# Fewer matmuls for the forget sums, a sixth PSUM bank for the odd projection, and a later wait for parameters in a hybrid encoder trunk

## What is computed

```python
logf = jax.nn.log_sigmoid((f_logit + b_f).astype(jnp.float32))
c_all = jnp.cumsum(jnp.concatenate([flogf_past.astype(jnp.float32), logf], axis=1), axis=1)
c_keys = c_all.transpose(0, 2, 1)[:, :, None, :]
c_q = c_all[:, P:]

def block(qp, qb, cqb):
    s = jnp.einsum('bqhd,bkhd->bhqk', qb, k_all).astype(jnp.float32)
    s = s + cqb.transpose(0, 2, 1)[..., None] - c_keys
    s = jnp.where(qp[:, None] >= kpos[None, :], s, NEG_INF)
    p = jax.nn.softmax(s, axis=-1).astype(v_all.dtype)
    return jnp.einsum('bhqk,bkhd->bqhd', p, v_all)
```

## Time and profile before

| | |
|---|---|
| three timed runs, us | 2606.72, 2608.28, 2618.82 (median 2608.28) |
| the profiled execution, us | 2615.28 |
| its span, us | 2613.2 |
| TensorE busy, us | 2454.7 (94%) |
| VectorE busy, us | 1699.5 (65%) |
| ScalarE busy, us | 1206.8 (46%) |
| mean granted clock of TensorE | 0.972 |

### The profile page before, as it was taken

The page is one execution under the profiler, slowest core; times in us unless marked ns, Lnnn a source line. Parts: engine busy times, 40 slices in busy tenths (PEclk is TensorE's granted clock), DMA queues, the critical chain, the costliest instruction groups (busy, mean ns, idle before and its releaser), DMA issues.

```text
span 2613.2 us, 37692 instructions
## 1 busy us (share of the span) xinstructions
PE 2454.7 (94%) x13907; PEld 2190.8 (84%) x13907; DVE 1699.5 (65%) x2809; ACT 1206.8 (46%) x2239; POOL 118.5 (5%) x177
## 2 busy tenths in 40 slices
PE   5999999998899899999989999999988898999998
PEld 5999987977767799988789998877777577999887
DVE  6777647676555877754687775474235858777546
ACT  5545435344344555543555553453224655554444
POOL 1000001100001000000100000010000010000000
PEclk9999999999899899999989999999997999999999
DMA  4233234421303232234522333343343042223335
GB/s 127 80 90 89 97 129 161 114 69 49 106 1 117 66 93 82 82 113 136 169 66 82 92 87 113 129 157 97 105 125 114 1 142 68 81 82 95 99 128 177
DMA packets 259140, 261.89 MB, mean 100 GB/s; under 512 B 25568, under 2 KB 214000, under 8 KB 258977
## 3 DMA queue, kind: packets, MB, share of 16 engines
q1 hardware_dynamic: 254224, 243.83, 31.1%
q0 software_dynamic: 4464, 14.80, 1.6%
q10 hardware_dynamic: 288, 1.10, 0.1%
HBM read 249.11 MB, written 10.58 MB: 99 GB/s over the span
## 4 chain that ended last, share of the span: by engine, by line
PE 78%; DVE 12%; ACT 4%; issue 3%; DMA 1%; POOL 1%; ACTq 0%; DVEq 0%; SPq 0%; POOLq 0%
PE ps L845 13%; PE ps L847 13%; PE ps L846 13%; PE ps L903 5%; PE ps L905 5%; PE ps L904 5%; PE ps L1311 3%; PE ps L1313 2%; PE ps L1312 2%; PE ps L962 2%; PE ps L964 2%; PE ps L963 2%; PE ps L1797 1%; PE ps L1501 1%; DVE xb L708 1%
## 5 line engine op out<-in xcount | busy, mean ns | idle before, releaser
L845 PE MATMUL ps<-xb,w_all 128*128 128x320 f32 x2400 | 752.3, 313 | 50.1 <-DVE w_all L592 29.4
L846 PE MATMUL ps<-xb,w_all 128*128 128x320 f32 x2400 | 749.0, 312 | 0.0
L847 PE MATMUL ps<-xb,w_all 128*128 128x320 f32 x2400 | 748.8, 312 | 0.0
L845 PEld LDWEIGHTS ps<-xb,w_all 128*128 128x128 f32 x2400 | 457.0, 190 | 58.3 <-issue 43.2
L492 DVE TENSOR_TENSOR w_all<-raw,w_all 128x1024 fp32r<-128x1024 f32 (+1 forms) x204 | 207.8, 1020 | 393.9 <-ACT w_all L502 212.6
L846 PEld LDWEIGHTS ps<-xb,w_all 128*128 128x128 f32 x2400 | 457.3, 191 | 0.0
L847 PEld LDWEIGHTS ps<-xb,w_all 128*128 128x128 f32 x2400 | 457.1, 190 | 0.0
L486 ACT ACTIVATE w_all<-raw 128x1024 fp32r<-128x1024 f32 (+1 forms) x204 | 182.4, 895 | 477.5 <-PE ps L905 254.8
L592 DVE TENSOR_TENSOR w_all<-raw,w_all 128x512 fp32r<-128x512 f32 x404 | 277.9, 690 | 147.1 <-ACT w_all L585 146.1
L585 ACT ACTIVATE w_all<-raw 128x512 fp32r<-128x512 f32 x404 | 253.2, 629 | 182.5 <-PE ps L847 139.2
L903 PE MATMUL ps<-w_all 128*128 128x512 f32 x528 | 205.9, 390 | 1.0 <-DVE w_all L507 1.0
(11 more groups left out here) (357 smaller groups left out, 3989.9 us busy)
## 6 DMA issues: line engine op xcount, KB each, us to landing
raw<-in_w_ffn_out SPq DMA_DIRECT2D x176, 512.0 KB, 3.4
raw<-in_w_ffn_in SPq DMA_DIRECT2D x120, 512.0 KB, 5.1
gain<-in_w_ffn_in SPq DMA_DIRECT2D x56, 512.0 KB, 5.0
raw<-in_w_in_odd SPq DMA_DIRECT2D x56, 256.0 KB, 2.7
raw<-in_w_out_even SPq DMA_DIRECT2D x16, 512.0 KB, 3.5
raw<-in_w_out_odd SPq DMA_DIRECT2D x16, 512.0 KB, 3.5
gain<-in_norm_g POOLq DMA_DIRECT2D x12, 512.0 KB, 7.3
raw<-in_w_in_even SPq DMA_DIRECT2D x24, 256.0 KB, 2.6
```

Source lines behind the costliest of these rows:

```text
L845: nc.tensor.matmul(dst, wl, xh[:, k, :], start=first, stop=False, skip_group_check=True)
L846: nc.tensor.matmul(dst, wh, xl[:, k, :], start=False, stop=False, skip_group_check=True)
L847: mm = nc.tensor.matmul(dst, wh, xh[:, k, :], start=False, stop=(k == HK - 1), skip_group_check=True)
```

## The change

It has three parts. First, the wait for `par_done` moves from behind the parameters' transposes to the place in front of the turning of tile 3, which writes bank 7. Second, the odd projection's blocks take their banks in turn from six (bank 7 is added), so a tile waits for the copy of the tile six places before it instead of five, and the loops are written out. Third, the forget sums of a head are made per key block alone, four matmuls; the sum of the blocks in front comes as a bias when ScalarE copies bank 6, so that copy is cut into four. These sums of the blocks in front, `nc_before`, are made once for all heads, by six matmuls more in `pe_cumulate` and a second copy of VectorE.

```diff
-        O_BANK = [0, 1, 4, 3, 2]
+        O_BANK = [0, 1, 4, 3, 2, 7]
...
                 if i == AHEAD:
+                    if f == 0:
+                        pe.wait_ge(par_done, 1)
                     pe_xt(pe, pre_, 3, 3)
...
-        def block_bank(name, t):
-            return bank(O_BANK[t] if name == "OT" else t)
+        def block_bank(name, b, t):
+
+            return bank(O_BANK[(5 * b + t) % 6] if name == "OT" else t)
...
+            for b in range(blocks):
                 for k in range(KD):
                     u = block_unit(name, first + b, k)
-                    pe.wait_ge(lo_done, reg(slot_no(u) + 1, it, KD))
+                    pe.wait_ge(lo_done, slot_no(u) + 1)
                     for t in range(NT):
-                        if k == 0:
-                            free(t)
-                        mm = block_tile(name, u, it, k, t)
+                        if k == 0 and start and b == 0:
+                            start(t)
+                        elif k == 0:
+
+                            pe.wait_ge(t_out, t0 + 5 * b + t + 1 - (6 if name == "OT" else 5))
+                        mm = block_tile(name, first + b, u, k, t)
...
                             for kb in range(NP):
-                                for b in range(kb + 1):
-                                    mm = nc.tensor.matmul(bank(6, P, kb * P), lgn[:, b, h:h + 1].to_broadcast([P, P]),
-                                                          con[:, C_UT:C_UT + P] if b == kb else ones,
-                                                          start=(b == 0), stop=(b == kb))
+                                mm = nc.tensor.matmul(bank(6, P, kb * P), lgn[:, kb, h:h + 1].to_broadcast([P, P]),
+                                                      con[:, C_UT:C_UT + P], start=True, stop=True)
...
-                        nc.scalar.activation(negc[:, h % 2, :], bank(6), ACT.Copy).then_inc(nc_done, 1)
+                            act.wait_ge(cq_done, 1)
+                        nc.scalar.activation(negc[:, h % 2, 0:P], bank(6, P), ACT.Copy)
+                        for kb in range(1, NP):
+                            e = nc.scalar.activation(negc[:, h % 2, kb * P:(kb + 1) * P], bank(6, P, kb * P), ACT.Identity,
+                                                     bias=nc_before[:, kb - 1, h:h + 1])
+                        e.then_inc(nc_done, 1)
...
+            for i in range(1, NP):
+                for b in range(i):
+                    mm = nc.tensor.matmul(bank(7, NH, 96 + (i - 1) * NH), ones, lgn[:, b, :], start=(b == 0), stop=(b == i - 1))
             mm.then_inc(cq_mm, 1)
...
-                    nc.vector.tensor_copy(cq, bank(7, NP * NH, 64).rearrange("p (t h) -> p t h", h=NH)).then_inc(cq_done, 1)
+                    nc.vector.tensor_copy(cq, bank(7, NP * NH, 64).rearrange("p (t h) -> p t h", h=NH))
+                    nc.vector.tensor_copy(nc_before, bank(7, (NP - 1) * NH, 96).rearrange("p (t h) -> p t h", h=NH))\
+                        .then_inc(cq_done, 1)
...
                 mm.then_inc(par_ps, 1)
-                pe.wait_ge(par_done, 1)
```

More of the change, by code:

```diff
@@ L226, in build_trunk @@
         cq = view(small, 480, NP, NH)
+        nc_before = view(small, 232, NP - 1, NH)
         h0a = small[:, 320:328]
@@ L1301, in block_unit, with block_tile @@
             return UNITS[name] + b * KD + k + (KD if name == "OT" and b else 0)
-        def block_bank(name, t):
-            return bank(O_BANK[t] if name == "OT" else t)
[L1306 to L1310, removed]
+        def block_bank(name, b, t):
+            return bank(O_BANK[(5 * b + t) % 6] if name == "OT" else t)
+        def block_tile(name, b, u, k, t):
+            wh, wl = w_slot(u, None, BW)
+            xh, xl = xt_lhs(u, None, k, t)
+            dst = block_bank(name, b, t)
             nc.tensor.matmul(dst, xl, wh, start=(k == 0), stop=False)
@@ L1335, in one @@
                         between(b * KD + k)
[L1336 to L1342, removed]
         def pe_first_block(pe, name, p):
@@ L1353, in pe_first_block @@
                     for t in TILES[g]:
-                        mm = block_tile(name, u, None, k, t)
+                        mm = block_tile(name, 0, u, k, t)
                         if k == KD - 1 and t < TILES[g][-1]:
@@ L1378, in act_block_out @@
                     act.wait_ge(t_mm, 4 * (t0 // 5 + b) + t + 1 - (1 if name == "OT" and (b or t > 2) else 0))
-                nc.scalar.activation(dest(t), block_bank(name, t), ACT.Copy, scale=scale).then_inc(t_out, 1)
+                nc.scalar.activation(dest(t), block_bank(name, b, t), ACT.Copy, scale=scale).then_inc(t_out, 1)
         def dve_units(dve, u0, count):
```

## The result

| | before | after |
|---|---|---|
| median of ten runs each on one chip, us | 2614.93 | 2628.32 |
| lowest to highest, us | 2606.72 to 2619.78 | 2625.35 to 2634.04 |
| the profiled execution, us | 2615.28 | 2625.35 |
| its span, us | 2613.2 | 2623.3 |
| TensorE busy, us | 2454.7 (94%) | 2475.9 (94%) |

What follows compares the result with a forecast made beforehand. TensorE bounds the kernel, with 78% of the span in the chain that ended last. -3.7 - 1.4 + 1.4 + 17.5 = +13.8, up to +15; 2608.3 + 14.5 = 2623 us, range 2596 to 2630.

Steps and rivals of the forecast that it cites:

- Part 1: Kernel start: the parameters' wait moves behind the first products, so the 48 matmuls start 4.0 us earlier; -3.7 us.
- Part 2: Odd projection: a sixth bank fills 0.69 us of the gap at block boundaries, two of which count; -1.4 us.
- The preparation: Before even attention: six small matmuls added when the sums are prepared; +1.4 us, 2.8 at the low clock.
- A head at the low clock: Even attention: a head at the low clock throughout after the change takes 14.1 us, against 10.3 before.
- case 1: Even attention: clock falls in head 1 and stays low to the end; heads together +17.5, whole 2623 us; chance 0.5.
- The pattern: Even attention: the granted clock falls in head 1 and stays low, as shorter forget sums neither restore nor hold it.
- The sum: Whole kernel: +13.8 us, up to +15 with low-clock preparation; 14.5 added to the median 2608.3 gives 2623 us.
- case 3: Even attention: clock comes back for some heads and falls again; 2600 to 2616, about 2608 us; chance 0.28.
- within half a per cent: Whole kernel: the outcome less than 13 us from before; chance 0.5, against 0.35 slower and 0.15 faster.
- The copies: Even attention: ScalarE's four 128-column copies for one of 512 cost +0.15 us a head, at most +0.45 without overlap.
- Case 2: Even attention: clock keeps its pattern or better; -14.0 us, 2594 us; chance 0.22, including copies that hide the sums' gain.

Runs made afterwards that it cites:

- parts 1 and 2 alone: The changed kernel with the forget sums as before, ten matmuls and one copy per head: 2607.51 us, ratio 0.9981 to the kernel before.
- part 3 alone: The kernel before with only the forget sums' hunks, their four copies and the small sums ahead: 2632.94 us, ratio 1.0080 to before.

## Why the prediction was right or wrong

- **Part 1, -3.7 us: right.** The first product moved from 25.98 to 21.32, -4.66 instead of -4.0 (its expected start was about 22.0), and the stage ends 4.93 earlier. The clock rose 5.1 us behind the first product instead of 4.1, later than the forecast 0.6, so the first 48 products end 4.24 earlier. One execution tells this only roughly: the ten experiments with parts 1 and 2 gave -2.3 to -4.4 at the first product, the run of parts 1 and 2 alone -3.2, and part 3 alone, which keeps the old wait, -0.6.
- **Part 2, -1.4 us: right, and for its reason.** Gaps of 0.57 to 0.59 instead of 1.36 and 1.27, and 0.73 and 0.72 more behind the two ropes: 2 x 0.78 + 2 x 0.68 - 1.45 is 1.5, and the projection's two marks give 1.45.
- **The preparation, +1.4 us: too small in the mean.** The twelve records themselves took 1.5 to 2.3 us in the seven kernels that have them. From the cumulated sums' first matmul to the first forget sum five kernels with the small sums and no filling ahead of head 0 took 61.3 to 64.6 us, mean 63.0, and six without the small sums 60.2 to 61.2, mean 60.7. That is 2.3, nearer to the 2.8 given for the low clock. But single executions differ more than that: in part 3 alone the stretch is 0.03 us longer than in before, in after 3.36, with the clock down from 630.5 to 637.4 (634.2 to 637.6 before) and from 681.7 on.
- **A head at the low clock, 14.1 us: right**, 14.00 in after and in part 3 alone.
- **The attention of case 1, +17.5: near.** Part 3 alone is this case: +15.6. Heads 0 and 1 gave -1.9 (forecast -2.3), head 2 +1.5 (+1.6), heads 3 to 6 +14.8 (+15.2). Head 7 was the miss, +1.2 against +3.0 to the output product.
- **The pattern.** The clock fell in head 1 as forecast, but in after it came back at 715.9 for heads 2 and 3, which gave 3.66 and 3.24 us back against 14.0 each. The tail was not in the sum: low clock in the first 3.5 us of the output product, +1.65.
- **The sum, +14.5, against 13.4 by the medians: right in size, in part by luck.** The 2623 us lie 5.3 below the measured median because the base moved by 6.65: three runs had a median of 2608.28, ten had 2614.93. And the items are not the sum's. In the profile of after, +10.07 in all, the attention costs 8.3 us instead of 17.5, and what makes up for it is the longer preparation and two stretches at the low clock that the sum did not have, +1.60 in the mixer's gates and +1.65 in the output product.
- **The step that failed is the one from the cases to the chances, and in it the price of case 3.** The prediction put half on "within half a per cent" while its likeliest case stood at 0.56% slower. It priced a clock that comes back for some heads at half of the way, 2608 us, and counted nearly all of that case as no difference. What the runs show in its place: the change is 0.59% slower, with an interval from 0.47% to 0.71%. The profile of after is case 3, for the clock came back for heads 2 and 3; that gave back 6.9 us of the forecast 17.5, and this execution is still 10.07 us slower. Part 3 alone is 0.80% slower, parts 1 and 2 give 0.19% back. The chance of slower by over half a per cent should have been the largest. Nor is half a per cent what a measurement of this kernel can just tell from no change: the intervals of after and of parts 1 and 2 alone are 0.12% to either side.
- **The reason was too narrow.** "The steps of a head without forget sums neither bring the high clock back nor hold it for long" fits after, but it is not the sums as such that are needed: transposes in a wait hold the clock as well, and ten matmuls with four copies lose it in many heads. The kernels that hold the clock better are those in which TensorE waits less in a head (each at or near the high clock): 0.33 us with ten transposes, 0.84 in before, which holds it for some heads, 1.30 with ten matmuls and four copies. That the wait decides is argued from this order; no run changes the wait and nothing else.
- **The copies, +0.15 to +0.45: 0.2** at the held clock; at the edge they cost 17 us (+12.6 against -4.1 by the medians, each against before), through the clock.
- **Case 2** (-14.0 us) is the size that the change with ten unread transposes has: 2597.19 us, -14.0 against before's median. But that is not the change's worth alone, for the transposes take time off without part 3 too: parts 1 and 2 are 4.1 us under before without them and 10.2 with them. Its heads of 9.2 us came at 9.48, with the transposes in them.

Open: what brings the clock back out of a low stretch in one execution and not in another. In 705.6 to 715.9 and in 729.5 to 777.3 of after TensorE is busy all the time; the clock rose after 10.3 us of the first, and not through 47.8 us of the second.

## What to carry to other kernels

Before taking matmuls out of a stage in which TensorE already waits, look at the granted clock of that stage: if it holds at 1.00 in some stretches and falls in others, the work that goes may cost more than it took. Here the 1.1 us that a head should have saved became 3.7 lost (10.3 against 14.0). When such an edit makes a kernel slower, put unread matmuls or transposes into the wait that ends a step; if the clock comes back the edit was good, and the filling may stay. Move a forecast to a base of many runs, and put the chances where the likeliest case's own number stands.

## What the runs showed of the hardware

- Ten transposes of 128x128 that nobody reads (1.25 us in each of seven heads) raised the mean clock of the profiled execution from 0.956 to 0.975 and took 27 us off (-14.0 against +13.4, each against before's median). Work that is not needed, 8.8 us of TensorE's time, paid for itself three times over.
- Four ScalarE copies of 128 columns in place of one of 512 cost 0.2 us a head with the clock held, and 17 us in all where it wasn't, though TensorE's own instructions were the same.
- Near the edge one kernel has many times: with three unread matmuls a head, runs from 2593.64 to 2642.09 us; with ten transposes, six runs within 4.1 us.
